# Part of the weight split of a two-layer decoder trunk is given to GpSimd

## What is computed

```python
for l in range(2):
    mod = silu(c) @ ada_w[l] + ada_b[l]              # (6 * 1024)
    sh1, sc1, gt1, sh2, sc2, gt2 = split(mod, 6)
    h = rms_norm(x, norm1_g[l]) * (1 + sc1) + sh1
    proj = h @ w_in[l]     # latents, dq, dk, dv, conv input, 3 * 1024 gates
    y_a = mla(rms_norm(q_lat) @ w_uq, rms_norm(kv_lat) @ w_ukv, k_rope) @ w_out_mla   # 8 heads
    y_b = rms_norm(diff_attention(dq, dk, dv)) @ w_out_diff                           # 4 heads
    y_c = silu(layer_norm(causal_dwconv31(a * sigmoid(g)))) @ w_out_conv
    x = x + gt1 * ((sigmoid(g0) * y_a + sigmoid(g1) * y_b + sigmoid(g2) * y_c) @ w_o)
    h = rms_norm(x, norm2_g[l]) * (1 + sc2) + sh2
    u = causal_dwconv3(h @ w_up)                     # (256, 2 * 2816)
    a, b = split(u, 2)
    x = x + gt2 * ((silu(a) * b) @ w_down)
return rms_norm(x, final_g)
```

## Time and profile before

| what | us |
|---|---|
| median of 3 runs | 1116.03 |
| lowest and highest run | 1115.15 and 1122.85 |
| the profiled execution's own time | 1116.03 |
| its span, first to last instruction | 1114.2 |
| TensorE (PE) busy | 1006.3 |
| VectorE (DVE) busy | 869.1 |
| ScalarE (ACT) busy | 515.3 |
| GpSimd (POOL) busy | 17.3 |

### The profile page before, as it was taken

One profiled execution on the slowest core, in us unless ns is written; L12 is line 12 of the kernel. 1 busy time (PEld: TensorE's weight loads), 2 busy tenths in 40 slices (PEclk: granted clock), 3 DMA queues, 4 the chain that ended last, 5 costly groups with the idle time before them and its releaser, 6 DMA issues.

```text
span 1114.2 us, 20254 instructions
## 1 busy us (share of the span) xinstructions
PE 1006.3 (90%) x7601; PEld 961.3 (86%) x7601; DVE 869.1 (78%) x1235; ACT 515.3 (46%) x715; POOL 17.3 (2%) x18
## 2 busy tenths in 40 slices
PE   2599999989888999999969999998997989999997
PEld 1598888989888999999969888898997989999996
DVE  5848989988696788898655898998869578888643
ACT  1644355437433554553345435543734355545432
POOL 6000000000000000000000000000000000000000
PEclk9898999889999899999989999987999989999998
DMA  9664443437656366657755444343666545564540
GB/s 318 239 189 152 124 131 100 153 104 249 241 195 222 115 207 221 218 188 299 265 178 187 155 124 126 105 148 109 229 232 220 185 145 199 196 218 155 187 152 38
DMA packets 138942, 201.07 MB, mean 180 GB/s; under 512 B 3416, under 2 KB 114148, under 8 KB 138852
## 3 DMA queue, kind: packets, MB, share of 16 engines
q1 hardware_dynamic: 138501, 199.63, 53.3%
q10 hardware_dynamic: 351, 0.26, 0.1%
HBM read 198.83 MB, written 1.05 MB: 179 GB/s over the span
## 4 chain that ended last, share of the span: by engine, by line
PE 62%; DVE 18%; issue 13%; ACT 2%; DMA 2%; SPq 1%; DVEq 1%; ACTq 0%
PE PB L1236 13%; PE PB L1237 12%; PE PB L1238 12%; DVE wL L838 4%; PE MI L1198 2%; PE SC L1236 2%; PE SC L1237 2%; PE SC L1238 2%; DVE buf L922 2%; DVE acc L793 2%; PE ST L1205 1%; DMA raw<-in_w_in 1%; DVE rdev L979 1%; PE SC L1337 1%; DVE xn L1025 1%
## 5 line engine op out<-in xcount | busy, mean ns | idle before, releaser
L1236 PE MATMUL PB<-hH,wH 128*128 128x256 f32 (+1 forms) x1568 | 467.8, 298 | 43.3 <-DVE hL L855 24.4
L1237 PE MATMUL PB<-hL,wH 128*128 128x256 f32 (+1 forms) x1568 | 451.8, 288 | 0.0
L1238 PE MATMUL PB<-hH,wL 128*128 128x256 f32 (+1 forms) x1568 | 451.5, 288 | 0.0
L838 DVE TENSOR_TENSOR wL<-raw,wH 128x2048 fp32r<-128x2048 f32 (+3 forms) x152 | 320.5, 2111 | 83.4 <-ACT wH L564 80.8
L1236 PEld LDWEIGHTS PB<-hH,wH 128*128 128x128 f32 (+1 forms) x1568 | 308.1, 197 | 57.2 <-issue 17.3
L564 ACT ACTIVATE wH<-raw 128x2048 fp32r<-128x2048 f32 (+3 forms) x152 | 266.4, 1769 | 132.1 <-DMA raw<-in_w_down 55.4
L1237 PEld LDWEIGHTS PB<-hL,wH 128*128 128x128 f32 (+1 forms) x1568 | 309.0, 197 | 3.3 <-issue 2.9
L1238 PEld LDWEIGHTS PB<-hH,wL 128*128 128x128 f32 (+1 forms) x1568 | 308.3, 197 | 0.0
L922 DVE SCALAR_TENSOR_TENSOR buf<-G,vec,buf 128x256 f32<-128x256 f32 x240 | 98.0, 477 | 0.3
L1075 DVE SCALAR_TENSOR_TENSOR cb<-PB,vec,cb 128x255 f32<-128x255 f32 (+1 forms) x88 | 36.3, 475 | 23.9 <-ACT cb L711 21.2
L796 DVE SCALAR_TENSOR_TENSOR acc<-ada,c_act,acc 128x1024 f32<-128x1024 f32 x40 | 51.4, 1284 | 2.3 <-DVE acc L793 1.2
(11 more groups left out here) (251 smaller groups left out, 1675.1 us busy)
## 6 DMA issues: line engine op xcount, KB each, us to landing
raw<-in_w_in SPq DMA_DIRECT2D x48, 1024.0 KB, 5.6
raw<-in_w_up SPq DMA_DIRECT2D x44, 1024.0 KB, 5.0
ada<-in_ada_w SPq DMA_DIRECT2D x40, 1024.0 KB, 5.7
raw<-in_w_down SPq DMA_DIRECT2D x22, 1024.0 KB, 5.0
ada_pre<-in_ada_w SPq DMA_DIRECT2D x8, 1024.0 KB, 11.6
raw<-in_w_o SPq DMA_DIRECT2D x8, 1024.0 KB, 6.2
raw<-in_w_out_diff SPq DMA_DIRECT2D x4, 1024.0 KB, 5.4
raw<-in_w_out_conv SPq DMA_DIRECT2D x4, 1024.0 KB, 6.0
```

The costliest lines, as they stand in the source:

```text
L838: dve.tensor_tensor(wL[s][:, 0:size], raw[s][:, 0:size], wH[s][:, 0:size].bitcast(F32), ALU.subtract).then_inc(w_lo[s], 1)
L1236: pe.matmul(out, a, xh(k), start=first and k == 0, stop=False, skip_group_check=True)
L1237: pe.matmul(out, a, xl(k), start=False, stop=False, skip_group_check=True)
L1238: ins = pe.matmul(out, b, xh(k), start=False, stop=last and k == kt - 1, skip_group_check=True)
```

## The change

GpSimd gets a function `low` of its own. For every chunk it waits for the same `w_hi` as VectorE and makes the columns from `cut` on; VectorE makes those before `cut`. The share of VectorE is 3/8 of the chunk's columns for n below `UP` and 4/8 from `UP` on. TensorE waits for both parts, by a second set of four semaphores. Nothing else moves; line numbers after the edits are larger by 7 to 24.

```diff
 RAW = 4
+SHARE, SHARE_UP = 3, 4
...
         w_lo = [sem(f"w_lo{i}") for i in range(RAW)]
+        w_lo_pool = [sem(f"w_lo_pool{i}") for i in range(RAW)]
...
+        def vector_share(n):
+
+            return chunk_size(n) * (SHARE_UP if n >= UP else SHARE) // 8
...
         @block.gpsimd
...
+            def low(l, n, r=0):
+
+                s, cut, size = n % RAW, vector_share(n), chunk_size(n)
+                pool.wait_ge(w_hi, l * CHUNKS + n + 1 + 4 * r)
+                pool.tensor_tensor(wL[s][:, cut:size], raw[s][:, cut:size], wH[s][:, cut:size].bitcast(F32),
+                                   ALU.subtract).then_inc(w_lo_pool[s], 1)
+
+            with pool.Fori(0, LAYERS) as l:
+                for n in range(UP + 2):
+                    low(l, n)
+                with pool.Fori(0, UP_LOOPS) as r:
+                    for j in range(4):
+                        low(l, UP + 2 + j, r)
+                for n in range(UP + 4 * UP_LOOPS + 2, CHUNKS):
+                    low(l, n)
...
         @block.vector
...
             def low(l, n, r=0):
 
-                s, size = n % RAW, chunk_size(n)
+                s, cut = n % RAW, vector_share(n)
                 dve.wait_ge(w_hi, l * CHUNKS + n + 1 + 4 * r)
-                dve.tensor_tensor(wL[s][:, 0:size], raw[s][:, 0:size], wH[s][:, 0:size].bitcast(F32),
+                dve.tensor_tensor(wL[s][:, 0:cut], raw[s][:, 0:cut], wH[s][:, 0:cut].bitcast(F32),
                                   ALU.subtract).then_inc(w_lo[s], 1)
...
             def split_ready(l, n, r=0):
 
                 after(w_lo[n % RAW], l * (CHUNKS // RAW) + n // RAW + 1 + r)
+                after(w_lo_pool[n % RAW], l * (CHUNKS // RAW) + n // RAW + 1 + r)
                 return wH[n % RAW], wL[n % RAW]
```

## The result

The changed kernel takes 1199.89 us in the median of 4 runs (1198.08 to 1201.65), against 1116.61 us before (4 runs, 1115.15 to 1122.85). The ratio is 1.0732, with a 95% interval of 1.07 to 1.0763: 83 us slower. The direction was forecast, the size was not: 1199.9 lies outside the range of 1088 to 1178.

A forecast was written before the change was run, and what follows sets the result against it. TensorE was taken to set most of the time, with VectorE its nearest rival. Up loop +13.6, layer 0's three further pairs +8, mixer +2.4 and output chunks +2 made +26 us on 1116: 1142 us, range 1088 to 1178.

The forecast's parts named there:

- turn-taking between two-input work of both engines: Two-SBUF-input VectorE work and two-input GpSimd work hold each other off nearly to the end; blocks of 2.7 or 2.2 us.
- some 390 us: GpSimd's added load: 152 subtractions of 2.9 and 2.4 us, so GpSimd is never the bound by its load.
- the mixer term: Mixer head pairs: VectorE saves 4.7 us, blocks cost 5.0, so +0.3 us a period, +2.4 us over both layers.
- safe list: VectorE work with one input in PSUM or only one tensor input, assumed to go on beside GpSimd without being held off.
- two-input rule: Only VectorE work with both inputs in SBUF (split, taps L922, ada products and others) is open to GpSimd's blocks.
- reading of GpSimd's one-input work: At the trace's start, GpSimd's one-input L518 cost L796 only 0.23 us, so no whole-length lock for one input.
- The bounds of the mixer: Per mixer period: -3 us if blocks lie wholly under other work, +4.6 us if never.
- Rival B: Relief wins: blocks fall mostly into VectorE's air and under PSUM work, TensorE's waits shrink; 1094 us, at best 1080; chance 0.25.
- The up loop: Up-projection turn of four chunks, 25.4 us before: +1.7 us taken from +1.2 to +3.3; eight turns make +13.6.
- The start: First chunks, put at 0 together with the norms, the end and the down-projection, where VectorE has little but splits.
- D: Nothing overlaps: mixer +36, loop +26, three pairs +10, outputs +8, so 1196 us, or 1178 with half the mixer's; chance 0.12.
- C: It cancels: the up loop loses some 10 us and the mixer gives as many back; 1116 us, chance 0.17.

The follow-up runs named there:

- relief: Changed kernel without GpSimd's part of the split, TensorE taking wH for the missing wL columns (times only, not a usable version): 1062.86 us, ratio 0.9518 to the kernel before.
- block_sub: Kernel before plus a dummy two-input GpSimd subtraction of 1024 columns behind 20 up-projection chunks per layer, no chunk waiting for it: 1163.33 us, ratio 1.0403.
- block_set: Kernel before plus a dummy write-only GpSimd memset of 2048 columns behind 20 up-projection chunks per layer: 1117.48 us, ratio 1.0005.
- nb_psum: Changed kernel with nmax, the 128x4 maxima that nb of L918 reads, in a PSUM bank instead of SBUF: 1205.22 us, ratio 1.0778 to the kernel before.
- block_one: Kernel before plus a dummy one-input GpSimd multiply-and-add of 1024 columns behind 20 up-projection chunks per layer: 1143.75 us, ratio 1.0246.
- up_only: Changed kernel with GpSimd's share only from UP (chunk 43) on, mixer and output chunks split by VectorE alone: 1154.74 us, ratio 1.0327 to the kernel before.
- second: Changed kernel with GpSimd's part of each chunk waiting for VectorE's part (w_lo in place of w_hi): 1195.71 us, ratio 1.0706 to the kernel before.

## Why the prediction was right or wrong

Right in their size were the durations. VectorE's bare 1.22 and 0.95 us are 1223 and 951 ns in relief. GpSimd's 2.9 and 2.4 us are 2.94 at 199.52 in the head pair and 2.40 at 455.07 in the up loop, where VectorE didn't hold them off. Right was the mechanism: turn-taking between two-input work of both engines, first told from the start of the trace, is shown by block_sub against block_set. PSUM taps unchanged, right. TensorE's second wait costs nothing of its own, right: 1.8 us. Its "some 390 us" for GpSimd is a slip: by its own 2.9 and 2.4 us the 152 subtractions make 374, and nothing in its sum hangs on it.

**The step that failed: the mixer term.** The prediction took one head pair, found +0.3 us, and multiplied it by 7.8. The pair itself came out at +0.5. The others did not: between score maxima the next two pairs of layer 0 lose 3.5 and 3.75 us, and the stretch ahead of the first one 6.9 (from 18.7 to 25.6). Of mixer and output chunks the forecast was +4.4 in both layers; they cost +42.6. That is 38 of the 58 us by which the forecast missed.

Cover doesn't explain why the chosen pair is cheap. Its reciprocal hides all but 0.56 us of one block (199.52 to 202.46), nearly as forecast. But the next pair has the same reciprocal (232.92 to 236.26), which hides all but 0.91 us of the same block (from 234.23), and it loses 3.5. What the costliest stretch shows is whom the block meets. The stretch before and after, as busy times, and one row of VectorE in it:

```profile
154.81:173.48 18.67, 17.64 (x135) 16.44 (x134) 17.80 (x38) 10.18 (x21) 0.00 (x0) 1.00 0.39 120
```

```profile
160.71:186.30 25.59, 21.11 (x137) 19.14 (x136) 20.18 (x39) 9.27 (x21) 7.91 (x3) 0.80 0.26 76
```

```profile
169.33 2.97 DVE L931 SCALAR_TENSOR_TENSOR W<-xn,rsum,W 128x128 f32<-128x128 f32 x1
```

L931 makes softmax weights, takes 0.34 us before the change, and TensorE stands still for its successor: the one wait for W in this stretch grows from 0.5 to 3.9 us. Nearly the same matmuls (137 against 135) are then busy 3.5 us longer at a granted clock of 0.80 instead of 1.00. So in this stretch the price of a block depends on whether TensorE waits for the instruction behind it, and the prediction's balance of VectorE's work (5.0 us of block against 4.7 saved) doesn't hold that. How the losses of the other stretches split up stays open. Before a period is multiplied, a second one has to be laid beside it.

**Its assumption on one-input work.** "One input in PSUM or only one tensor input" was put on the safe list. For the first half it holds. For the second it holds for the reciprocals (L1002 stays at 3341 ns); the maxima (L916, 414 ns as before) read PSUM and belong to the first. It doesn't hold for tensor_scalar from SBUF to SBUF: nb went from 170 to 2181 ns, and L814, a product of 1024 columns, from 745 to 1690 ns. The Trainium skill, "SBUF — State Buffer", section "Who interferes with whom", lists tensor_scalar and copies among the operations that can take the shared ports; this case's rows agree. The prediction used its two-input rule alone. This carries less of the miss than the 35 us of L918 suggest, since nb_psum took that row away and gained nothing.

**Its reading of GpSimd's one-input work.** From L518 at the start, beside which L796 lost only 0.23 us, the prediction took it that a one-input operation of GpSimd holds VectorE off less than for its whole length. The one-input dummy of block_one does hold it off to 0.2 us before its end. The two operations differ and what sets them apart was not tried. The sum doesn't use this reading, since all of GpSimd's new work has two inputs.

**The bounds of the mixer.** "TensorE's own 30.88 against 34.0 forbids more", behind the bound of -3 us, took a busy time at a granted clock of 0.90 for fixed. In relief the same 216 matmuls are busy 27.71 us at 1.00 and the pair is 5.4 us shorter. Rival B's best, 1080, was too dear by 17: relief reaches 1063, so the listed waits of TensorE are not the whole price of being late. Over the span the clock stood at 0.965 in relief, 0.956 before and 0.927 after, in the order of the times; how much of the loss goes through it was not separated by a run.

**The up loop, by its terms.** The half turn with the ada product was forecast at 15.1 us and lasts 15.3; the other half, forecast at 11.5 to 12.3, lasts 12.7, so this turn is +2.6 where +1.7 was taken from +1.2 to +3.3. It is again the cheapest of its kind. By the starts of VectorE's splits the four turns of layer 0 last 28.0, 28.0, 29.1 and 30.0 us (100.5 in all before, 115.1 after), those of layer 1 together 114.7 against 100.5. Eight turns cost +28.8 where 13.6 was forecast, 3.6 each, which is above the upper bound of 3.3. The rest of the two stages, 38.2 - 28.8 = 9.4 us, was forecast as 8 in layer 0 alone: there it is 6.0, and layer 1 loses 3.4 outside its turns, where nothing was put.

**The start** costs 3.8 us where 0 stood. Two instructions of VectorE meet GpSimd's first two subtractions there. The split of 768 columns at 42.79 takes 3.68 us where the whole split took 2.29, and behind it stands a copy from SBUF to SBUF that took 0.35 us before:

```profile
46.48 2.95 DVE L1115 COPY vec<-vec_all 128x384 f32 x1
```

In up_only, where the first chunks are not shared, both are back at 2.29 and 0.35 us and the first norm starts at 47.1 us.

Of the rivals D came nearest in number (1178 to 1196), and in its parts: 44 for mixer and outputs (42.6 measured), 36 for the up loop (38.2). Its reason, that nothing overlaps, is not what the trace shows, since blocks lie under the reciprocals; its number holds no term for TensorE's lower clock, so that the sum fits is in part luck. Its chance of 0.12 was too small: its condition, the sum of VectorE's work and blocks above the period, was met by its own figures (36 against 34 us). C is excluded by the stages, B as a whole by the 225.6 us of VectorE's lengthening. What B priced, the relief, was there in full and more.

## What to carry to other kernels

Work handed from VectorE to GpSimd is not free because GpSimd is: here every us of reading on GpSimd put half a us on VectorE, and a us taken from VectorE gave back only a third. Before moving anything, list which of VectorE's instructions in that stretch read one operand from PSUM, release GpSimd together with those and make its piece hardly longer than they are; 768 columns (1.85 us) under 1.65 us of taps gained 0.66%, 1024 gained nothing, and the same 768 released a moment early lost 1.8%. Ask of each block which instruction it will meet and who waits for that one. And a period chosen for a hand calculation needs a second one beside it: both of mine, the head pair and the turn, were the cheapest of those that I compared afterwards.

## What the runs showed of the hardware that I had not expected

- A block is kept: with one victim out of its way (nb_psum) it moves to the next instruction open to it, VectorE's busy time stays (931.5 against 930.4 us) and the time gains nothing (1205.2 against 1199.9).
- An instruction of four elements, L918, is held off as long as one of a thousand: 2181 ns in the mean, 2.69 us at 187.48 where GpSimd's subtraction had begun at 187.20. So is a copy from SBUF to SBUF (2.95 us at 46.48, bare 0.35).
- A write-only operation of GpSimd holds nothing off (1.81 us of memset, forty times, ratio 1.0005).
- A one-input operation of GpSimd can hold VectorE off as wholly as a two-input one: to 0.15 to 0.22 us before its end in block_one, 0.14 to 0.21 in block_sub. It costs less because it is shorter (1.04 against 1.89 us for the same columns).
- The loss exceeds what VectorE's durations show: 25.6 us against 14.1 more busy time in block_one, 45.2 against 38.0 in block_sub. What makes up the rest stays open.
- Gapless work of VectorE can keep GpSimd waiting to its end: in second a subtraction of 2.94 us, issued at 198.50, ended at 205.52, behind eight taps and a split. It doesn't always: in the change GpSimd's 320 columns, issued at 229.74 in the middle of eight taps, took 1.13 us, and the tap that they met took 1.10 instead of 0.47. What decides was not tried.
